# Value sums of the paged decode in two PSUM banks by turns, and an order of units of its own for ScalarE

## The reference, cut to what matters

```
q, k, v, u = split(rmsnorm(x) @ w_in);  rotary on q, k
prompt:  s = q k^T (2 score sets for each of 4 heads), causal softmax
         a = p0 - lam * p1;  o = a @ v;  o = rmsnorm(o)
decode:  the same against cache_k[page_table], cache_v[page_table]
s5_mix:  a diagonal state-space scan over u, gelu, gate
x += [attn, s5] @ w_out
x += top-2-of-8 experts in the best of 4 groups (32 gated MLPs)
y  = rmsnorm(x)
```

## Time and profile before

| | |
|---|---|
| time, median of 3 runs | 1522.09 us (1521.27 to 1523.09) |
| the profiled execution: time, span | 1525.98 us, 1524.3 us |
| granted TensorE clock, mean | 0.923 of full speed |
| busy: PE, DVE, ACT, POOL | 1307.3, 522.8, 247.9, 212.9 us |
| moved by DMA | 458.35 MB, 301 GB/s on average |

### The profile page before, as it was taken

How to read it: one execution, slowest core, us unless ns; L and a number is a source line. 1 busy time by engine, 2 the same in 40 slices (tenths; PEclk the granted TensorE clock), 3 DMA queues, 4 the chain that set the end, 5 groups by cost and what they waited for, 6 DMA issues and landing times.

```text
span 1524.3 us, 26488 instructions
## 1 busy us (share of the span) xinstructions
PE 1307.3 (86%) x8952; PEld 686.1 (45%) x8952; DVE 522.8 (34%) x1430; ACT 247.9 (16%) x473; POOL 212.9 (14%) x327
## 2 busy tenths in 40 slices
PE   4899899999878877999877999986789999999930
PEld 2455565654424334666663434343344444444410
DVE  1452334443375354554431111134221211111227
ACT  2100111121112122332321000000011111111111
POOL 1102104041300200000010000000122222222111
PEclk9899999999898889999899999986899999999975
DMA  9499989889788976898897979897979999999854
GB/s 356 172 322 297 318 271 305 317 249 324 244 274 273 334 274 233 313 344 312 275 325 287 330 248 336 293 317 254 359 278 356 366 368 364 360 351 357 299 180 195
DMA packets 186454, 458.35 MB, mean 301 GB/s; under 512 B 24177, under 2 KB 24561, under 8 KB 177778
## 3 DMA queue, kind: packets, MB, share of 16 engines
q1 hardware_dynamic: 165906, 394.41, 73.6%
q0 software_dynamic: 20448, 62.59, 12.6%
HBM read 421.92 MB, written 33.80 MB: 299 GB/s over the span
## 4 chain that ended last, share of the span: by engine, by line
PE 67%; DMA 11%; DVE 9%; SPq 4%; issue 4%; DVEq 2%; ACT 1%; POOL 1%; ACTq 0%; POOLq 0%; PEldq 0%
PE WA L1756 48%; PE SC L1756 10%; PE OD L1756 4%; DMA ring<-in_cacheK 3%; DMA qpad<-h_scratch,idc 3%; SPq L484 2%; DMA ring<-in_cacheV 2%; PE WA L2098 2%; DMA arena<-in_x_s 1%; SPq L472 1%; DVE st L1100 1%; DMA ring<-h_scratch,idc 1%; PE WA L1857 1%; DVE arena L1725 1%; DVE arena L1738 1%
## 5 line engine op out<-in xcount | busy, mean ns | idle before, releaser
L1756 PE MATMUL WA<-arena 128*128 128x512 f32 (+10 forms) x1440 | 358.0, 436 | 26.2 <-issue 14.1
L1756 PE MATMUL WA<-arena,xm 128*128 128x512 f32 (+2 forms) x768 | 312.4, 610 | 7.6 <-DMA arena<-in_w_out 5.5
L1756 PEld LDWEIGHTS WA<-arena 128*128 128x128 f32 (+2 forms) x1440 | 196.7, 200 | 160.7 <-issue 138.3
L1756 PEld LDWEIGHTS WA<-arena,xm 128*128 128x128 f32 (+1 forms) x768 | 122.3, 179 | 160.7 <-issue 153.1
L1756 PE MATMUL SC<-ring,sall 128*32 128x512 f32 x1024 | 141.1, 671 | 35.8 <-DVEq L1183 21.9
L1756 PE MATMUL WA<-xm,arena 128*128 128x512 f32 x192 | 89.1, 612 | 1.7 <-ACT arena L931 1.3
L548 POOL TENSOR_TENSOR st<-st,consts 128x1 f32<-128x1 f32 (+2 forms) x18 | 13.8, 764 | 496.0 <-DVEq L1134 310.9
L1756 PEld LDWEIGHTS SC<-ring,sall 128*32 128x32 f32 x1024 | 28.0, 116 | 118.3 <-issue 66.6
L1756 PE MATMUL OD<-ring,qpad 128*32 128x128 f32 x2048 | 68.0, 286 | 10.5 <-DMA ring<-in_cacheK 10.4
L799 ACT ACTIVATE arena<-WA,st 128x128 f32<-128x128 f32 (+7 forms) x64 | 47.4, 741 | 146.5 <-DVEq L1104 146.5
L1756 PE MATMUL SC<-ring,qpad 128*32 128x128 f32 x2048 | 67.5, 286 | 3.8 <-DMA ring<-in_cacheK 3.8
(11 more groups left out here) (351 smaller groups left out, 1234.8 us busy)
## 6 DMA issues: line engine op xcount, KB each, us to landing
ring<-in_cacheK SPq DMA_DIRECT2D x512, 256.0 KB, 4.6
ring<-in_cacheV SPq DMA_DIRECT2D x512, 256.0 KB, 4.6
arena<-in_w_gu SPq DMA_DIRECT2D x16, 2048.0 KB, 10.0
arena<-in_w_dn SPq DMA_DIRECT2D x16, 1024.0 KB, 14.4
ring<-in_w_gu SPq DMA_DIRECT2D x8, 2048.0 KB
xm<-in_w_gu SPq DMA_DIRECT2D x8, 2048.0 KB, 10.4
arena<-in_w_in SPq DMA_DIRECT2D x32, 256.0 KB, 10.1
ring<-in_w_dn SPq DMA_DIRECT2D x8, 1024.0 KB
```

Of the source, the lines that this page charges most:

```text
L1756: return pe.matmul(out, lhsT, rhs, start=first, stop=last, **kw)
```

## The change

Value sums: even sequences are summed in `SC`, odd ones in `OD`. DVE's copy and weights move from `ov` to the last part of the last V unit of a sequence. `ov` keeps PE's four products, now into columns 260 to 263 of the sequence's own bank, and DVE's copy to `aD`; in the plan it comes behind `V(x, y+1, 0, 1)`. V's first unit of sequence y no longer waits for `s_o4`: y = 0 waits for the transposed exponentials as before, y = 1 for DVE's reciprocal of the row totals (which are in `OD`), y = 2 and 3 for the `s_ad` of sequence y - 2. The row totals and their reciprocal move into `pt`, behind its first four transposes.

ACT's order: ACT walks through `ACT_PLAN`, which is `PLAN` sorted by the end of each unit on the planner's clock, with 2.4 added for the units S. The exponentials of S thus stand behind ACT's copies of units that end up to 2.4 later on that clock.

```diff
--- before.py
+++ after.py
@@ -91,11 +91,11 @@
             b = SPP * x + y
             for t in range(TURNS):
                 for g in range(2):
-                    late = [(("pt", x), 1.2)] if t + g + y == 0 else [(dec[-2][0], 1.2)] if t + g == 0 else []
+                    late = [(("pt", x), 1.2)] if t + g + y == 0 else [(("ov", b - 2), 1.2)] if t + g == 0 and y >= 2 else []
                     dec.append((("V", x, y, t, g), 1.95, late))
-                    if t + g == 0 and y:
-                        dec[-1], dec[-2] = dec[-2], dec[-1]
-            dec.append((("ov", b), 0.4, [(("V", x, y, TURNS - 1, 1), 1.5)]))
+                    if y and t == 0 and g == 1:
+                        dec.append((("ov", b - 1), 0.5, [(("V", x, y - 1, TURNS - 1, 1), 2.5)]))
+        dec.append((("ov", b), 0.5, [(("V", x, y, TURNS - 1, 1), 2.5)]))
     dec += [(("dout",), 0.1, [(("ov", NB - 1), 1.0)]), (("dout2",), 0.2, [(("dout",), 2.0)]),
             (("out", NT), 4.0, [(("dout2",), 1.0), (("out", NT - 1, 1, 1), 0.0)]), (("hn", NT), 0.0, [(("out", NT), 2.0)]),
             (("hs", NT), 0.0, [(("hn", NT), 2.5)]), (("hT", NT), 1.0, [(("hs", NT), 0.8)]),
@@ -227,7 +227,7 @@
-    return plan
+    return plan, end
@@ -250,8 +250,13 @@
     ALU, ACT, AX = mybir.AluOpType, mybir.ActivationFunctionType, mybir.AxisListType.X
     MUL, ADD, SUB, MAX, MIN = ALU.mult, ALU.add, ALU.subtract, ALU.max, ALU.min
 
-    PLAN = [u + x for u in make_plan() for x in ([(p,) for p in range(PARTS)] if u[0] in ("K", "V") else [()])]
+    order, ends = make_plan()
+    PLAN = [u + x for u in order for x in ([(p,) for p in range(PARTS)] if u[0] in ("K", "V") else [()])]
     SPOT, USES = banks(PLAN)
+
+
+    ready = {u: ends.get(u, ends.get(u[:-1], 0.0)) + (2.4 if u[0] == "S" else 0.0) for u in PLAN}
+    ACT_PLAN = sorted(PLAN, key=lambda u: ready[u])
 
     POW = {}
     for unit in PLAN:
@@ -385,7 +390,7 @@
         SC = ctx.enter_context(nc.psum_tensor("SC", [128, 512], f32))
         OD = ctx.enter_context(nc.psum_tensor("OD", [128, 512], f32))
-        nkP, mxT, mbP, lP, aP = OD[0:32, 0:NB], OD[0:1, 128:256], OD[:, 256:257], OD[:, 257:258], OD[:, 260:264]
+        nkP, mxT, mbP, lP = OD[0:32, 0:NB], OD[0:1, 128:256], OD[:, 256:257], OD[:, 257:258]
         WA = ctx.enter_context(nc.psum_tensor("WA", [128, 512 * BANKS], f32))
         W = [WA[:, 1024 * i:1024 * i + 1024] for i in range(3)]
 
@@ -916,7 +921,7 @@
             todo = {"stats": stats, "dqkv": dqkv, "dprep": dprep, "k": k, "kt": kt, "v": v, "q": q, "qt": qt, "S": S, "T": T,
                     "ot": ot, "m3": m3, "K": K, "pt": pt, "s5a": s5a, "bP": bP, "bK": bK, "bX": bX, "bY": bY, "bG": bG,
                     "glu": glu, "hn": hn, "pick2": pick2}
-            for unit in PLAN:
+            for unit in ACT_PLAN:
                 if unit[0] in todo:
                     todo[unit[0]](*unit[1:])
 
@@ -1170,19 +1175,22 @@
                 dve.wait_ge(s_pexp, x + 1)
                 dve.tensor_tensor(mrow[:, 2:3], mrow[:, 2:3], mrow[:, 3:4], ADD)
                 dve.drain().then_inc(s_l, 1)
-
-            def ov(b):
-                x, y = divmod(b, SPP)
-                if y == 0:
-                    dve.wait_ge(s_lP, x + 1)
-                    dve.reciprocal(mrow[:, 4:5], lP)
-                    dve.drain()
-                dve.wait_ge(s_pv, b + 1)
-                dve.tensor_copy(o4s[:, :], SC[:, :])
+                dve.wait_ge(s_lP, x + 1)
+                dve.reciprocal(mrow[:, 4:5], lP)
+                dve.drain().then_inc(s_l, 1)
+
+            def Vv(x, y, r, g, p):
+
+                if r < TURNS - 1 or g == 0 or p < PARTS - 1:
+                    return
+                dve.wait_ge(s_pv, SPP * x + y + 1)
+                dve.tensor_copy(o4s[:, :], (SC, OD)[y % 2][:, :])
                 dve.tensor_scalar(wmap[:, SPP, :], wmap[:, y, :], mrow[:, 4:5], None, MUL)
                 dve.drain().then_inc(s_o4, 1)
+
+            def ov(b):
                 dve.wait_ge(s_aP, b + 1)
-                dve.tensor_copy(aD[:, :, b], aP)
+                dve.tensor_copy(aD[:, :, b], (SC, OD)[b % 2][:, 260:264])
                 dve.drain().then_inc(s_ad, 1)
 
             def dout():
@@ -1674,7 +1682,7 @@
-"pt": pt, "ov": ov,
+"pt": pt, "V": Vv, "ov": ov,
...
@@ -1923,33 +1931,37 @@
                         last = pe.transpose(slot("PT", x, n)[:, 128 * j:128 * j + 128],
                                             sall[:, n, 128 * j:128 * j + 128], ident)
                     last.then_inc(full_sem("PT", x, n), 1)
+                    if n == 0:
+                        pe.wait_ge(s_l, 2 * x + 1)
+                        mm(lP, consts[:, C_SUM:C_SUM + 128], mrow[:, 2:3]).then_inc(s_lP, 1)
                 vacant(pe, "PTn", x)
                 pe.transpose(slot("PTn", x)[0:NB, 0:128], snew[:, :], ident).then_inc(full_sem("PTn", x), 1)
-                pe.wait_ge(s_l, x + 1)
-                mm(lP, consts[:, C_SUM:C_SUM + 128], mrow[:, 2:3]).then_inc(s_lP, 1)
 
             def Vv(x, y, r, g, p):
+                acc = (SC, OD)[y % 2]
                 if r + g + p == 0:
-                    if y:
-                        pe.wait_ge(s_o4, SPP * x + y)
+                    if y == 0:
+                        pe.wait_ge(s_ptw, x + 1)
+                    elif y == 1:
+                        pe.wait_ge(s_l, 2 * x + 2)
                     else:
-                        pe.wait_ge(s_ptw, x + 1)
+                        pe.wait_ge(s_ad, SPP * x + y - 1)
                 landed(x, SPP * UPB + UPB * y + 2 * r + g, g, p)
                 for j in range(p, GRP, PARTS):
 
                     t, q, c = j // 2, j % 2, j // 2
                     blk = sall[:, r, 256 * g + 128 * q:256 * g + 128 * q + 128]
-                    last = mm(SC[32 * c:32 * c + 32, :], blk[:, 32 * t:32 * t + 32], ring[:, GRP * g + j, :],
+                    last = mm(acc[32 * c:32 * c + 32, :], blk[:, 32 * t:32 * t + 32], ring[:, GRP * g + j, :],
                               r + g + p == 0, r == TURNS - 1 and g == 1 and p == PARTS - 1 and c > 0,
                               skip_group_check=True)
                 last.then_inc(s_pgfree, 1)
                 if r == TURNS - 1 and g == 1 and p == PARTS - 1:
-                    mm(SC[0:32, :], ptn[:, 0:32], dv[:, :], False, True, skip_group_check=True).then_inc(s_pv, 1)
+                    mm(acc[0:32, :], ptn[:, 0:32], dv[:, :], False, True, skip_group_check=True).then_inc(s_pv, 1)
 
             def ov(b):
                 pe.wait_ge(s_o4, b + 1)
                 for h in range(H):
-                    last = mm(aP[:, h:h + 1], o4s[:, 128 * h:128 * h + 128], wmap[:, SPP, h:h + 1])
+                    last = mm((SC, OD)[b % 2][:, 260 + h:261 + h], o4s[:, 128 * h:128 * h + 128], wmap[:, SPP, h:h + 1])
                 last.then_inc(s_aP, 1)
 
             def dout():
```

More of the change, by code:

```diff
@@ L1676, in _ @@
             todo = {"stats": stats, "dqkv": dqkv, "dprep": dprep, "u": u, "k": k, "q": q, "S": S, "C": C, "O": O, "AN": AN,
-                    "m1": m1, "m2": m2, "m3": m3, "pt": pt, "ov": ov, "dout": dout, "dout2": dout2, "s5a": s5a, "bA": bA, "bK": bK,
+                    "m1": m1, "m2": m2, "m3": m3, "pt": pt, "V": Vv, "ov": ov, "dout": dout, "dout2": dout2, "s5a": s5a, "bA": bA, "bK": bK,
                     "bE": bE, "bH": bH, "bY": bY, "bG": bG, "glu": glu, "out": out_, "hn": hn, "hs": hs, "hT": hT,
```

## The result

| | before | after |
|---|---|---|
| median, same chip | 1522.59 us (4 runs) | 1476.22 us (1471.05 to 1478.94, 4 runs) |
| ratio | | 0.9684, 95% interval 0.9646 to 0.9722 |
| profiled execution: time, span | | 1475.24 us, 1473.5 us |
| granted clock, PE busy | | 0.938, 1284.7 us |

Beside later experiments the same kernel was timed twice more, against the kernel before on the chip of each: 1483.26 against 1522.57 us (0.9742, interval 0.9711 to 0.9773) and 1479.66 against 1518.45 us (0.9761, interval 0.9728 to 0.9795). So the gain is 39 to 46 us by the medians, with the first measurement at the upper end. The direction and the likeliest mechanism were right; the forecast gain was about half of the measured one.

The account below looks back on a forecast made before the run. PE's fixed order was taken to bound the first part, with waits for DVE's copy. Gains of 22.4 + 7 = 29.4 us, less 6.9 for landing waits, gave 22.5: 1522.1 to 1499.6 us, own range 1490 to 1510, eight-in-ten range 1485 to 1519.

Parts of the forecast that it names:

- value sums: banks and early copy: Removing PE's waits for DVE's copy of the value sums at changes of sequence: 22.4 us gained.
- the landing waits: PE's waits for V pages to land, 13.8 us in nine places, were let grow by half: 6.9 us lost.
- the plan turns: The greedy plan may shift single units on the changed costs: no sign known, 5 us to either side.
- 1.7 us for each such row: First V unit behind a gap runs at the lower clock, 3.64 us against 1.93: 1.7 us counted for each.
- seven gaps: PE's waits or delays at 388.63, 453.18, 515.30, 586.85, 894.89, 956.52 and 1009.77 us; gains summed to 22.4 us.
- the first gap: At 388.63 us: 4.28 us idle, 1.7 of clock, 0.8 in the products; gain 6.8 us, bounds 0 and 6.8.
- the seventh gap: At 586.85 us, fourth sequence: PE's products waited 3.10 us for the copy; gain 3.1 us, bounds 0 and 3.1.
- the second gap: At 453.18 us: 6.92 us idle and 1.7 of clock, DVE late with the scan; gain 2.0 us, bounds -4 and 8.6.
- The last change of sequence: Sign to check, second pass: at 1009.77 us before, it should come near 987.
- the 3 us that I had set as a warning: If DVE's waits for PE at the copy pass 3 us on average and C or AN waits grow equally, the forecast falls.
- rival B: Slower: DVE waits in line at each sequence's last V unit, costing 39 us against 29.4 gained; 1532 us, chance 0.10.
- Rival D: All of it: each gap counts whole with its clock, no landing wait grows; 41.5 us gained, 1481 us, chance 0.08.

Follow-up runs that it names:

- e1: Both banks and the early copy on the old plan, ACT in that plan's order, against the kernel before: 1496.13 us, ratio 0.985.
- e12: New plan and ACT's order, value sums as before (one bank, copy in `ov`), against the kernel before: 1513.27 us, ratio 0.994.
- e11: The whole change timed again, against the kernel before on the same chip: 1483.26 us, ratio 0.974.
- e2: ACT's order alone, put on the kernel before: 1507.01 us, ratio 0.9905.
- e16: The whole change without ACT's order, timed a second time, against the kernel before: 1486.25 us, ratio 0.9776.
- e15: The whole change timed once more on another chip, against the kernel before: 1479.66 us, ratio 0.9761.
- e4: The whole change without ACT's order (ACT walks `PLAN`), against the kernel before: 1482.70 us, ratio 0.976.
- e3: The planner's new costs alone, put on the kernel before, value sums and ACT as before: 1518.89 us, ratio 0.9975.
- e7: Banks without ACT's order, plan new up to the first unit of sequence 2 and old after, against the kernel before: 1501.13 us, ratio 0.986.
- e8: Banks without ACT's order, plan new up to the second pass's K units and old after, against the kernel before: 1486.47 us, ratio 0.977.
- e5: Banks and ACT's order on the old plan, against the kernel before: 1484.80 us, ratio 0.975.
- e6: The whole change with one bank, copy still early, against the kernel before: 1483.49 us, ratio 0.974.
- e9: The whole change with two banks but DVE's copy back in `ov`, against the kernel before: 1489.39 us, ratio 0.979.
- e10: The whole change with `C(0,3)` moved before the scan `bH(3)` on DVE alone, against the kernel before: 1488.59 us, ratio 0.978.
- e13: The whole change with PE made to wait idle for POOL behind three sums of the second pass: 1504.51 us.
- e14: The whole change with PE doing useless matmuls behind three sums of the second pass, POOL's added work running unwaited: 1504.50 us.

## Why the prediction was wrong

| step of the sum | forecast, us | measured, us |
|---|---|---|
| value sums: banks and early copy, less the landing waits | 22.4 - 6.9 = 15.5 | 23 on the old plan (e1; interval 16 to 31), 30 on the new (e12 to e11) |
| ACT's order | 7 | 14 on the old plan (e2), 6.6 on the new, not told from none (e16 to e15) |
| the plan turns | 0, "5 us to either side" | 13.4 with the banks (e1 to e4), 4, not told from none, without (e3) |
| in all | 22.5 | 23 + 13.4 + 6.6 = 43; whole change 46, 39 and 39 |

**The steps that failed.** The first is "The greedy plan may turn on the changed costs ... I know no sign for this and give it 5 us to either side". It was worth 13.4 us, and it isn't added on top like a constant: without the banks it gave 4 us that can't be told from none (e3). The plan and the value sums help each other: by the medians the value sums' edit is worth 22 us on the old plan (e1), and 36 (e3 to e4) and 30 (e12 to e11) on the new. The prediction had no term for that. Which of the planner's shifts does it stays open; they lie between sequence 2 of the first pass and the second pass's K units (e7 to e8).

The second is the clock inside the 22.4 us: "I count 1.7 us for each such row". I counted it at three of seven gaps, 5.1 us, and 0.8 us for the products. Behind the first gap alone the rows of before lost 5.1 us, and behind the second the next V unit, at 460.77, again took 3.64 us. In the profiles, the four kernels that keep the waits for the copy (before, e2, e3, e12) have PE busy for 1297 to 1310 us, 1303.9 on average; the twelve others without added work have 1276 to 1290, 1284.7 on average. Of these 19.2 us, 11.7 lie in the two stretches between the sums of one pass, where the six waits of V stood, 2.0 for each; 5.8 lie between the last sum of the first pass and the first of the second, where the seventh gap was, and why it is so much there isn't shown. The rest, 1.7, lies ahead of all of them.

**The landing waits, which came and went.** "I let them grow by half, 6.9 us" looks wrong in the whole change: V pages were waited for 13.8 us before and 13.6 after (16.5 and 16.6 in e11 and e15), K pages 14.2 and 16.2. But wherever the value sums' edit alone was put on, the wait for V pages did grow: 13.8 to 19.6 us (before to e1), 14.3 to 17.7 (e2 to e5), 7.5 to 13.1 (e3 to e4) and 9.2 to 16.5 (e12 to e11), 5.5 on average. It was the new plan that took as much away: 13.8 to 7.5 (before to e3), 19.6 to 13.1 (e1 to e4), 14.3 to 9.2 (e2 to e12). So the term was right for the edit it was meant for, and the plan hid it. The 23 us of e1 are what is left after it, and stand against 15.5, not against 22.4; that both are near 22 is chance.

**The idle time in e1.** In e1 the span of the profile fell by 30 us, of which 23 are busy time and only 7 idle, since AN was waited for 10.7 us more and V pages 5.8 more. At the second gap I had kept 2.0 us of 8.6, and it was about -2.

**What was right.** The waits for the copy fell to 0.9 ("about 1"), V took 1.92 us at the first changes and 3.64 at the last, "issue" fell to 7.1 ("about 7"), the clock rose. The last change of sequence came at 971.90, not near 987: the early mark of what had been missed. DVE waited 3.6 us on average for the sum at its copy, past the 3 us that I had set as a warning, but C and AN grew only by 5.4 and 1.6 us, so rival B, slower, had its place and not its price. Rival D, all of it, came nearest (1481 us, chance 0.08), though not in its way: the second gap did not count whole, and a third of the gain came from the plan, which D has at nothing.

**What spoke against the second bank.** "Adding PSUM double-buffering gave no further gain", says the Trainium skill ("TensorE: Matmul & The Clock Gate", section on HAM oscillation), of a matmul kernel that had already been reordered against its waits for DMA. It fits what e6 shows of the second bank by itself: with the copy early, one bank gives 0.974 and no wait of V for the copy. I had taken it to speak against the whole edit. With the copy late (e12 to e9) the second bank, with `ov` one V unit later, was worth 23.9 us here, so the sentence doesn't carry over to that case.

## What to carry to other kernels

When in-order engines share one list and a drain stands late in it, move the drain to the earliest place in the waiting engine's own order before adding a buffer. When an edit changes a cost that a greedy planner reads, the new order is an edit of its own: list what it moves, and give it a range as wide as that of any other part. When you price a gap of PE, read all the rows behind it until they are back at their usual times, not only the next one, and in several profiles.

## What the runs showed of the hardware

- The cost in clock of a gap isn't set by its length: 4.28 us idle cost 5.1 us in the rows behind it (before), 3.98 us idle in e10 cost 8.5, and behind the same gap of 5.9 us the first group took 4.83, 5.32 and 6.48 us in three executions of one kernel, where it takes 3.60 at full clock.
- Idling against working, in three places: 26.0 us idle took as long as 34.3 us of matmuls (e13, e14).
- Between executions of one kernel time goes with the granted clock: over 147 executions of the kernels here, within each kernel, 0.001 of mean clock went with about 1.3 us (correlation -0.80). One kernel's executions spread over 4 to 21 us, so a difference of 5 us can't be told from six executions of each, even side by side on one chip.
- The whole change, profiled three times, had spans of 1473.5, 1485.6 and 1470.2 us with PE busy 1284.7, 1284.7 and 1276.1. The 12.1 us between the first two are waiting: 3.3 us for pages, 5.9 for other transfers, the rest spread.
